# Moving the loads of a DRAM staging loop to SyncE's queue, the loads of a split activation to GpSimd's, and spilling each split piece in one transfer

## The reference

```python
h = _rmsnorm(x, norm1[l])
proj = jnp.einsum('bsd,de->bse', h, w_in[l])
(u_pool, c_b, c_c, c_x, q, k, v, qi, ki, wi, gate_logits) = jnp.split(proj, pts, axis=-1)
a = _multiscale_pool(u_pool, pool_w[l], pool_scale[l])
bconv = _short_conv(c_b, c_c, c_x, conv_w[l])
q, k = _rmsnorm(q, q_gain[l]), _rmsnorm(k, k_gain[l])          # 8 heads of 128
c = _sparse_attention(q, k, v, qi, ki, wi * IDX_HEADS ** -0.5, topk)   # 128 keys of each token
g = jax.nn.sigmoid(gate_logits).reshape(B, S, N_BRANCH, D)
merged = (g[:, :, 0] * (a @ w_pool_out[l]) + g[:, :, 1] * (bconv @ w_conv_out[l])
          + g[:, :, 2] * (c @ w_attn_out[l]))
x = x + merged @ w_o[l]
h2 = _rmsnorm(x, norm2[l])
f = jnp.square(jax.nn.relu(h2 @ w_ff1[l]))                     # width 8192
x = x + f @ w_ff2[l]
```

## Time and profile before

| | |
|---|---|
| median of 3 runs | 2753.04 us (2750.91 to 2757.0) |
| the profiled execution | 2753.44 us |
| its span in the trace | 2751.6 us |
| PE busy | 2666.3 us, 97% |
| DVE busy | 2013.1 us, 73% |
| ACT busy | 1232.1 us, 45% |
| POOL busy | 98.5 us, 4% |
| queue q1 (SP) | 426.82 MB |
| queue q10 (ACT) | 73.54 MB |
| queue q0 (POOL) | 50.34 MB |
| mean granted PE clock | 0.99 of full speed |

### The profile page before, as it was taken

How to read it: one execution, slowest core, us unless ns; L and a number is a source line. 1 busy time by engine, 2 the same in 40 slices (tenths; PEclk the granted TensorE clock), 3 DMA queues, 4 the chain that set the end, 5 groups by cost and what they waited for, 6 DMA issues and landing times.

```text
span 2751.6 us, 37283 instructions
## 1 busy us (share of the span) xinstructions
PE 2666.3 (97%) x14614; PEld 2304.4 (84%) x14614; DVE 2013.1 (73%) x2347; ACT 1232.1 (45%) x1591; POOL 98.5 (4%) x124
## 2 busy tenths in 40 slices
PE   7998999999999999999998999999999899999998
PEld 6686798777888888888888999999998788888887
DVE  8575644546777777556777888888887788888787
ACT  5322232334544444234465666566565333333332
POOL 4011111000000000000000000000000000000000
PEclk9999999999999999999999999999999999999999
DMA  4476757435655446745673655665668667675843
GB/s 138 155 232 211 252 176 253 134 119 202 226 169 162 153 158 199 263 158 199 222 245 108 215 178 183 215 203 173 215 211 322 242 241 269 210 291 168 312 151 109
DMA packets 313272, 552.98 MB, mean 201 GB/s; under 512 B 19536, under 2 KB 134864, under 8 KB 313104
## 3 DMA queue, kind: packets, MB, share of 16 engines
q1 hardware_dynamic: 276352, 426.82, 47.0%
q10 hardware_dynamic: 22928, 73.54, 7.1%
q0 software_dynamic: 13824, 50.34, 5.4%
HBM read 433.05 MB, written 117.44 MB: 200 GB/s over the span
## 4 chain that ended last, share of the span: by engine, by line
PE 77%; DVE 9%; DMA 8%; issue 4%; ACT 1%; POOL 1%; SPq 0%; ACTq 0%; DVEq 0%; POOLq 0%
PE main L1231 7%; PE main L1232 7%; PE main L1233 7%; PE aux L1129 7%; PE aux L1131 7%; PE aux L1130 7%; PE main L1129 5%; PE main L1131 5%; PE main L1130 5%; DMA group<-w_ff 3%; PE main L488 3%; PE main L490 2%; PE main L489 2%; DMA t_dram<-stage 2%; DVE f_wl L2051 1%
## 5 line engine op out<-in xcount | busy, mean ns | idle before, releaser
L1231 PE MATMUL main<-sf,f_wh 128*128 128x256 f32 x1728 | 491.7, 285 | 9.7 <-DVE cf_low L2537 6.0
L1232 PE MATMUL main<-sf,f_wh 128*128 128x256 f32 x1728 | 491.4, 284 | 0.0
L1233 PE MATMUL main<-sf,f_wl 128*128 128x256 f32 x1728 | 491.3, 284 | 0.0
L1231 PEld LDWEIGHTS main<-sf,f_wh 128*128 128x128 f32 x1728 | 333.9, 193 | 10.1 <-DVE cf_low L2537 6.2
L1232 PEld LDWEIGHTS main<-sf,f_wh 128*128 128x128 f32 x1728 | 333.8, 193 | 0.0
L1233 PEld LDWEIGHTS main<-sf,f_wl 128*128 128x128 f32 x1728 | 333.8, 193 | 0.0
L458 ACT ACTIVATE w_hi<-w_raw 128x512 fp32r<-128x512 f32 (+1 forms) x184 | 113.1, 616 | 330.1 <-PE main L490 240.0
L488 PE MATMUL main<-act_hi,w_hi 128*128 128x512 f32 (+1 forms) x528 | 216.9, 411 | 23.2 <-DVE w_lo L465 23.2
L465 DVE TENSOR_TENSOR w_lo<-w_raw,w_hi 128x512 fp32r<-128x512 f32 (+1 forms) x184 | 129.7, 708 | 148.4 <-ACT w_hi L458 146.6
L1418 ACT ACTIVATE f_wh<-group 128x1024 fp32r<-128x1024 f32 x128 | 135.6, 1061 | 217.3 <-PE aux L1131 87.0
L1129 PE MATMUL aux<-f_wh,sf 128*128 128x512 f32 x512 | 201.2, 393 | 10.3 <-DVE f_wl L2051 5.7
(11 more groups left out here) (285 smaller groups left out, 6182.1 us busy)
## 6 DMA issues: line engine op xcount, KB each, us to landing
group<-w_ff SPq DMA_DIRECT2D x160, 512.0 KB, 5.0
f1raw<-w_ff SPq DMA_DIRECT2D x128, 512.0 KB, 5.8
sf<-f_dram ACTq DMA_DIRECT2D x56, 1024.0 KB, 11.9
group_g<-w_in SPq DMA_DIRECT2D x100, 512.0 KB, 4.5
w_raw<-w_in SPq DMA_DIRECT2D x88, 512.0 KB, 4.7
f_dram<-piece_hi SPq DMA_DIRECT2D x112, 256.0 KB, 4.0
f_dram<-piece_lo SPq DMA_DIRECT2D x112, 256.0 KB, 5.2
t_dram<-stage POOLq DMA_DIRECT2D x48, 512.0 KB, 3.9
```

The costliest lines, as they stand in the source:

```text
L1231: pe.matmul(part, hi_at(8, k)[:, cols], sh, start=first, stop=False, skip_group_check=True)
L1232: pe.matmul(part, hi_at(8, k)[:, cols], sl, start=False, stop=False, skip_group_check=True)
L1233: mm = pe.matmul(part, lo_at(8, k)[:, cols], sh, start=False, stop=last, skip_group_check=True)
```

## The change

Four things are changed.

- The loads of the staging are issued by SP (`load_stage`), not by POOL. They stand between the loads of `w_raw`: round s of 0 to 7 behind load 6 + 4 s of the qk stage, rounds 8 and 9 behind loads 8 and 13 of the v stage, 10 and 11 behind loads 1 and 4 of the stage after it. SP's two hardware loops over these loads are written out, so that the new loads can stand between them. POOL keeps the stores.
- DVE does the differences of rounds 0 to 7 one step later, in the steps 5, 6 and 7 of a pass, the last two both in step 7. Rounds 8 to 10 are in the steps 9 to 12, 17 to 20 and 25 to 28 of the v stage.
- `load_s` is issued by POOL, behind the stores of the staging, with the same conditions; ACT issues none of these transfers any more.
- The high and the low part of a piece lie in one tensor (at the same addresses as before), and `spill_f` writes both with one transfer of 512 KB, which adds 16 to `f_spilled` in place of 32.

```diff
+            def load_stage(s):
+                J, g, h = (0, 6, 7)[s // 4], s % 4, s // 8
+                w, c0 = (w_in, c_gate) if J == 0 else (w_o, (J - 6) * S)
+                if s == 0:
+                    sp.wait_ge(score_added, 24)
+                    sp.wait_ge(score_mm, 24)
+                else:
+                    sp.wait_ge(stage_mixed, 4 * s)
+                    sp.wait_ge(stage_stored, 64 * s)
+                if s == 8:
+                    sp.wait_ge(topk_done, 1)
+                for b in range(4):
+                    r0, col = (b // 2) * (D // 2) + 2 * g * P, c0 + b % 2 * (D // 2)
+                    sp.dma_start(stage[h][b][:], w[r0:r0 + 2 * P, col:col + S].rearrange("(k p) c -> p k c", p=P)
+                                 ).then_inc(stage_landed, 16)
+            for l in range(8 * LP):
+                load(u_qk // 2 + l, l % RAWS, w_in, l % LP * 2 * UK * P, l // LP * COLS + c_q)
+                if l >= 6 and (l - 6) % LP == 0:
+                    load_stage((l - 6) // LP)
+            for l in range(4 * LP):
+                load(u_v // 2 + l, l % RAWS, w_in, l % LP * 2 * UK * P, l // LP * COLS + c_v)
+                if l == 2:
+                    load_stage(7)
+                if l == 8:
+                    load_stage(8)
+                if l == 13:
+                    load_stage(9)
...
+                    if l in (1, 4):
+                        load_stage(10 + l // 4)
...
-                for hl, piece in ((0, piece_hi[o % PIECES]), (1, piece_lo[o % PIECES])):
-                    sp.dma_start(f_dram[q // 4, S_SLOT[idx], hl, :, (q % 4) * S:(q % 4 + 1) * S],
-                                 piece[:].bitcast(F32)).then_inc(f_spilled[o % PIECES], 16)
+                sp.dma_start(f_dram[q // 4, S_SLOT[idx], :, :, (q % 4) * S:(q % 4 + 1) * S].rearrange("l p c -> p l c"),
+                             piece[o % PIECES][:].bitcast(F32)).then_inc(f_spilled[o % PIECES], 16)
...
-                if n % UP >= 4:
-                    mix_stage(n // UP, n % UP - 4)
+                if n % UP >= 5:
+                    mix_stage(n // UP, n % UP - 5)
+                if n % UP == UP - 1:
+                    mix_stage(n // UP, 3)
...
-                if 11 <= n < 29 and (n - 11) % 7 < 4:
-                    mix_stage(8 + (n - 11) // 7, (n - 11) % 7)
+                if n % 8 in (1, 2, 3, 4) and 8 < n:
+                    mix_stage(8 + n // 8 - 1, n % 8 - 1)
...
+            for n in range(7):
+                load_s(0, n, 28 * 8 + 14 * (F1_PAIRS - 1) + 2 * n + 2)
+            for c in range(1, 4):
+                it = 2 * c - 1
+                for n in (0, 1):
+                    load_s(c, n, K2 + 28 * it + 8)
+                for n in (4, 3, 2):
+                    load_s(c, n, K2 + 28 * it + 20)
+                for n in (5, 6):
+                    load_s(c, n, K2 + 28 * it + 28)
```

More of the change, by code:

```diff
@@ L160, in build @@
         cf = cf_low[:, :, :]
-        piece_hi = [at(f"piece_hi{i}", [P, S], F32R, (144 + 4 * i) * KB) for i in range(4)]
-        piece_lo = [at(f"piece_lo{i}", [P, S], F32R, (146 + 4 * i) * KB) for i in range(4)]
+        piece = [at(f"piece{i}", [P, 2, S], F32R, (144 + 4 * i) * KB) for i in range(4)]
+        piece_hi, piece_lo = [a[:, 0, :] for a in piece], [a[:, 1, :] for a in piece]
         group = [at(f"group{i}", [P, 2, 2, S], F32, o * 512) for i, o in enumerate((144, 208, 176))]
@@ L1754, in act_after @@
                     square_f(q, 0)
[L1756 to L1763, removed]
-                                  ).then_inc(s_landed[n], 16)
             hi1(0, 0, 0)
@@ L2723, in _ @@
             for s in range(12):
-                J, g, h = (0, 6, 7)[s // 4], s % 4, s // 8
-                w, c0 = (w_in, c_gate) if J == 0 else (w_o, (J - 6) * S)
-                if s == 0:
-                    pool.wait_ge(score_added, 24)
-                    pool.wait_ge(score_mm, 24)
-                if s == 8:
-                    pool.wait_ge(topk_done, 1)
-                if s:
-                    pool.wait_ge(stage_mixed, 4 * s)
-                    pool.wait_ge(stage_stored, 64 * s)
-                for b in range(4):
-                    r0, col = (b // 2) * (D // 2) + 2 * g * P, c0 + b % 2 * (D // 2)
-                    pool.dma_start(stage[h][b][:], w[r0:r0 + 2 * P, col:col + S].rearrange("(k p) c -> p k c", p=P)
-                                   ).then_inc(stage_landed, 16)
+                g, h = s % 4, s // 8
                 for i, b in enumerate((0, 1, 3, 2)):
@@ L2742, in _, with load_s @@
                                    ).then_inc(stage_stored, 16)
+            def load_s(c, n, freed):
+                for s in range(PIECES):
+                    pool.wait_ge(f_spilled[s], 16 * ((28 * (c + 1) - s + PIECES - 1) // PIECES))
+                pool.wait_ge(g_done, freed)
+                for h in range(2):
+                    pool.dma_start(sf[h][n].rearrange("p l k c -> p l (k c)").bitcast(F32),
+                                   f_dram[c, n, :, :, h * 2 * S:(h + 1) * 2 * S].rearrange("l p c -> p l c")
+                                   ).then_inc(s_landed[n], 16)
+            for n in range(7):
[8 more added lines that the diff above has]
+                    load_s(c, n, K2 + 28 * it + 28)
 def constants(norm1, norm2, pool_scale, conv_w, q_gain, k_gain):
```

22 lines of the change are left out of this document (4 added, 18 removed).

## The result

The changed kernel takes 2715.64 us (median of 4 runs, 2714.37 to 2718.37), the kernel before 2754.19 in the same comparison (2750.91 to 2757.0): ratio 0.9862, 95% interval 0.9845 to 0.9879, so 38.5 us less. The forecast was 2717 with a range of 2703 to 2733. The profiled execution took 2718.37 us, its span is 2716.6.

The account below looks back on a forecast made before the run. PE bounds the kernel, busy 97%, losing time where the staging ring (26.8 us) outlasts its pass (21.7). 2753.4 - 40.2 (staging) + 4 (v stage) + 0 + 0 = 2717 us; overall range 2703 to 2733, the forecast's own 2711 to 2724.

Parts of the forecast that it names:

- the size of the loss: Stretches from 150 to 350 and 450 to 500 us: 27.7 us idle plus 12.5 by the clock, 40.2 to win.
- The ring of store, loads and differences: Staging in the qk stage: one round takes 26.8 us, 5.1 longer than PE's pass of 21.7.
- The fourth load: POOL's staging loads: the fourth shows 5.63 us of "issue", about the time three loads need to land, not POOL's work.
- The rival that SP's queue would have the same gap: Staging: the fourth load is late on SP too, the round stays, 2753 us; chance 0.03.
- The new round: Staging in the qk stage: 7.2 us loads, 6.3 differences, 5.5 last store, 19.0 in all, 2.7 under the pass.
- the rival of longer landings: Staging: loads and stores each land some 2.2 us later, a round takes 23.5 us, total 2730 us; chance 0.15.
- the named signs: DVE's waits for stage loads fall from 81.7 us to under 20; SP's waits for stores are under 2 us.
- The v stage: Rounds 9 and 10: DVE stands some 4.5 us each; 4 us taken for this and the first round, bounds 0 to 18.
- Spill and ACT at nothing: One 512 KB spill: 0 us, bounds +-1; moving 56 loads of 1 MB from ACT to POOL: 0.
- The end of F1 at nothing: Stall of 18.3 us (11.7 idle, 6.6 clock) keeps its size: 0 taken, between -18 and +12.
- The rival of a smaller stall: End of F1: POOL's loads leave SP gaps, two thirds of 18.3 us saved, 2705 us; chance 0.10.
- The rival of a greater stall: End of F1: POOL's queue gets more than its turn, PE idle 24 us instead of 11.7, 2729 us; chance 0.06.

Follow-up runs that it names:

- more memory: Kernel before with GpSimd's descriptor memory at 1536 bytes a partition instead of 1024, nothing else changed: 2727.38 us, ratio 0.9904.
- the earlier rounds: Changed kernel with SP's loads of stage rounds 9 and 10 one weight load earlier: 2711.53 us, ratio 0.9851 to the kernel before.
- the light loads: Changed kernel with the first 14 loads of split f cut to a quarter of their columns (output not the reference's): 2698.68 us, ratio 0.9796.
- the staging alone: Kernel before with SP's stage loads, the differences' new places and POOL only storing; split f and its spill as before: 2721.35 us, ratio 0.9881.
- the loads by SP: Kernel before with stage loads issued by SP, POOL only storing, DVE's differences in their old places: 2729.19 us, ratio 0.9907.
- the new places: Kernel before with DVE's differences in their new units; POOL still issues loads and stores: 2732.89 us, ratio 0.9925.

## Why the prediction was right, step by step

**What bounds, and the size of the loss.** Right. The ring of store, loads and differences was longer than the pass; each of three ways to shorten it (SP's loads, the order of the differences, more memory for descriptors) took 20 to 26 us off, and none of them changes what PE computes. The loss was put at 27.7 us idle and 12.5 by the clock, 40.2. After the change these same stretches have 0.46 us idle at a clock of 1.00. But 27.7 and 12.5 are not what was won: over the whole span the idle time fell by 24.6 us and PE's busy time by 10.4.

**The fourth load.** The prediction read the 5.63 us as a wait until three loads have landed and left its cause unnamed; the run with 1536 bytes names it. The rival that SP's queue would have the same gap fell with the first trace: four issues in 2.06 us, with no gap.

**The new round.** The idea was right, the size was off, and by more than the turn first shown suggests. In that turn it is 8.5 us from issue to first difference, not 7.2, because the last stage load lands after 6.96 us and not 5.8; the differences and the store are nearly as reckoned, and the turn is 20.3 us, not 19.0. The mean turn is 21.8 us (21.3 in the second trace). What was left out is POOL's wait ahead of a store, where the prediction had 0.3 us for each issue: the two waits alone make 6.4 us over seven turns, 0.9 of the 1.5 us by which the mean lies above the turn shown. So of the margin of 2.7 us under the pass 0 to 0.4 is left in the mean. With a ring as long as the pass, the stock of three units takes up the turns that are longer. That PE shows nothing of it was partly luck, and the rival of longer landings was closer than its 13 us of distance made it look. Whether the changed kernel with 1536 bytes for descriptors gets its margin back was not run.

**DVE's and SP's waits.** Here the named signs failed though the sum held. DVE's waits were to fall under 20 us: they are 52.3. SP's for stores were to be under 2 us: they are 22.4. Both have one reason. In the qk stage SP waited for the stores in every round after the first, so that each turn began when the one before it had ended: the ring still goes round at its own pace, and DVE, which is done with its other work, waits for the loads 2.9 to 6.2 us in each round. The 8 us of stock in front of PE and the 19 us by which SP's weight loads run ahead cover this, as the prediction had reckoned in the same paragraph. The sign to name was PE's idle time, not DVE's.

**The v stage.** 4 us taken, bounds 0 to 18. Measured from 350 to 500 us: 4.3 idle and 1.5 by the clock, 5.8 us. 3.0 of them are the small product of the pool branch that was named (PE at L986, waiting for br_lo of L2024, behind round 9's stage wait of 5.7 us, where 4.5 was reckoned; the 9.4 us, which the expectation of the earlier rounds put there, is round 10's), 1.3 a low part. The two earlier rounds take both away.

**Spill and ACT at nothing.** Right for each alone (ratios 0.9996 and 0.9998); beside the new staging up to 5 us are open. That later quarters need no more than three loads in flight holds: POOL's waits ahead of these loads that nothing but "issue" explains are 142.1 us, 20 of them, and PE never waits for a block of split f.

**The end of F1 at nothing.** Right for the change: 17.0 us lost in the three stretches against 18.3. The reason given, that the change moves no bytes out of a full stretch, is what the light loads show. The rival of a smaller stall rested on a gap between POOL's loads; but with three transfers of 1 MB in flight the engines were as full as with ten, at 1.03 to 1.04 before and after. The rival of a greater stall leaned on the Trainium skill ("DMA: Bandwidth & Descriptors", section "Queues, rings and completion order"), by which an engine drains a whole packet of several descriptors before it turns to the next queue. Here the software queue moved 1148 packets of 3.9 KB and the hardware queue 1758 of 1.9 KB in 20 us, 4.43 and 3.39 MB. That is 1.3 times the bytes, where ACT's hardware queue had 1.6 times: the longer packets go with more bytes, and that POOL issues them gives its queue no greater share. Whether the profile's packets are those of the page, no row says.

**The sum.** 2753.4 - 40.2 + 4 = 2717 against 2718.37 in the profiled run and 2715.64 in the median. The closeness of the median is in part luck. The staging was to give 36.2 us and gave 31.9 by itself; the full change gave 38.5, and the 6 us or so between the two, forecast as nothing, lie in the part that scatters.

## What to carry to other kernels

When a chain of waits goes round, measure several turns, not one, and the pass of the engine that it runs beside. What counts is the difference between the two: a shorter ring pays until the busiest engine no longer waits for it, and then there is nothing left to win, so do the cheapest edit first (here one number, the memory for software descriptors, gave 25.9 us, where the whole change gave 38.5) and don't add up gains of edits that work on the same ring. When DMA is full in a stretch, moving transfers within it moves the stall (2714.2 us here against 2715.64); taking bytes out of it removed it (15.0 us). Putting them into its gaps gained by the times (ratio 0.9806 against 0.9851), but no trace shows where.

## What the runs showed of the hardware

- With 1024 bytes for descriptors POOL's fourth load of 512 KB waited 5.6 to 7.6 us; with 1536 the four went in 2.90 us. In the changed kernel, where POOL issues stores alone in the qk stage, one at 193.93 us waits 4.65 us and, seven stores later, one at 238.39 us 4.44 us, each until about 5 us after the store ahead of it, the time that a store needs to land; of the 1 MB loads, where three go together, the fourth waits 7.6 to 9.6 us. At 214.48 us a fourth store goes without a wait, as long after the three ahead of it as the one that waited would have, so the limit is not simply a number in flight. That the stores' waits too come from the memory for descriptors is inferred from the loads; what exactly the memory frees, and when, was not tried.
- With the idle time came a gain by the clock of 0.4 to 0.5 of it (9.8, 6.8, 6.4 and 8.8 us of busy time beside 22.7, 16.6, 13.7 and 16.9 idle, in the runs of the staging alone, the loads by SP, the new places and more memory). In the stretches of the qk stage with 5.9 to 9.4 us idle of 50 it was granted at 0.90 to 0.98 of full speed, with under 0.7 idle at 1.00. So 22.7 us of idle time were worth 32.
- The scatter between runs of the changed kernel (2711.6 to 2718.4 us) stands, in the one pair of traces, mostly where DMA is full: of 5.9 us between them, 4.8 are in 100 us at the end of F1. Another 2.2 us of idle time are in F2 from 2350 to 2650 us. What starts it was not shown.
